# One silu and one product for both token tiles of a feed-forward block, with the roundings, sums and transfers around them reordered

## The reference

```python
def swiglu(u, w_in, w_out):
    gate, up = jnp.split(u @ w_in, 2, axis=-1)
    return (jax.nn.silu(gate) * up) @ w_out
...
    h = h + 0.5 * g1 * swiglu(u, ffn_w_in[l, 0], ffn_w_out[l, 0])
    ...
    h = h + g2 * hybrid_mixer(u, ...)
    ...
    h = h + 0.5 * g3 * swiglu(u, ffn_w_in[l, 1], ffn_w_out[l, 1])
```

## Time and profile before

| what | value |
|---|---|
| median of 3 runs | 1303.82 us |
| profiled execution | 1307.19 us |
| its span | 1305.4 us |
| granted TensorE clock, mean | 0.942 |
| TensorE busy | 1192.3 us, 91% |
| VectorE busy | 869.4 us, 67% |
| ScalarE busy | 467.9 us, 36% |
| transfers | 253.70 MB, 194 GB/s in the mean |

### The profile page before, as it was taken

One profiled execution on the slowest core, in us unless ns is written; L12 is line 12 of the kernel. 1 busy time (PEld: TensorE's weight loads), 2 busy tenths in 40 slices (PEclk: granted clock), 3 DMA queues, 4 the chain that ended last, 5 costly groups with the idle time before them and its releaser, 6 DMA issues.

```text
span 1305.4 us, 13525 instructions
## 1 busy us (share of the span) xinstructions
PE 1192.3 (91%) x5163; PEld 891.6 (68%) x5163; DVE 869.4 (67%) x1579; ACT 467.9 (36%) x833; POOL 25.9 (2%) x30
## 2 busy tenths in 40 slices
PE   3889999589989988999987999995998998999998
PEld 2668888456556566888866888872575655788887
DVE  6877776646676677777467687854476776755553
ACT  2434443101154544444344344411112453634441
POOL 7000000000000000000000000000000000000000
PEclk9989999887969998999998999997977899999999
DMA  9898896155511018877348888833653010576641
GB/s 357 287 332 307 313 335 238 45 171 142 185 35 65 33 51 304 297 281 275 126 165 289 311 321 312 311 129 125 150 177 125 33 33 33 194 237 215 216 155 65
DMA packets 153461, 253.70 MB, mean 194 GB/s; under 512 B 9639, under 2 KB 128053, under 8 KB 145205
## 3 DMA queue, kind: packets, MB, share of 16 engines
q1 hardware_dynamic: 152692, 251.53, 56.1%
q10 hardware_dynamic: 704, 1.30, 0.3%
HBM read 251.76 MB, written 1.05 MB: 194 GB/s over the span
## 4 chain that ended last, share of the span: by engine, by line
PE 79%; DVE 10%; DMA 6%; SPq 2%; issue 1%; ACT 1%; DVEq 0%; ACTq 0%
PE ps L581 10%; PE ps L583 10%; PE ps L582 10%; PE ps L686 10%; PE ps L602 7%; PE ps L604 7%; PE ps L606 7%; DMA tall<-in_ffn_w_out_dram 4%; PE ps L564 4%; PE ps L796 2%; PE ps L731 2%; PE ps L593 2%; PE ps L706 1%; PE ps L705 1%; DVE h L1348 1%
## 5 line engine op out<-in xcount | busy, mean ns | idle before, releaser
L581 PE MATMUL ps<-wh,uh 128*128 128x512 f32 x640 | 252.6, 395 | 0.0
L583 PE MATMUL ps<-wlo,uh 128*128 128x512 f32 x640 | 249.5, 390 | 0.0
L582 PE MATMUL ps<-wh,ul 128*128 128x512 f32 x640 | 249.2, 389 | 0.0
L1325 DVE TENSOR_TENSOR wlo<-wide,wh 128x1024 fp32r<-128x1024 f32 x176 | 204.9, 1220 | 6.7 <-ACT wh L953 6.7
L953 ACT CAST wh<-wide 128x1024 fp32r<-128x1024 f32 x176 | 173.2, 1050 | 23.5 <-DMA wide<-in_ffn_w_in_dram 23.5
L686 PE MATMUL ps<-wide,u 128*128 128x512 f32 (+2 forms) x320 | 130.0, 567 | 28.7 <-issue 28.7
L602 PE MATMUL ps<-th,fh 128*128 128x512 f32 x352 | 144.3, 410 | 5.7 <-DVE fl L1360 5.7
L1354 DVE TENSOR_TENSOR tlo<-tall,th 128x1024 fp32r<-128x1024 f32 x104 | 123.3, 1221 | 27.2 <-ACT th L960 26.5
L604 PE MATMUL ps<-th,fl 128*128 128x512 f32 x352 | 141.3, 401 | 0.0
L606 PE MATMUL ps<-tlo,fh 128*128 128x512 f32 x352 | 141.0, 401 | 0.0
L583 PEld LDWEIGHTS ps<-wlo,uh 128*128 128x128 f32 x640 | 120.1, 188 | 25.6
(11 more groups left out here) (255 smaller groups left out, 1371.0 us busy)
## 6 DMA issues: line engine op xcount, KB each, us to landing
wide<-in_ffn_w_in_dram SPq DMA_DIRECT2D x176, 512.0 KB, 5.1
ada<-in_ada_w_dram SPq DMA_DIRECT2D x60, 1024.0 KB, 7.7
tall<-in_ffn_w_out_dram SPq DMA_DIRECT2D x44, 1024.0 KB, 6.4
wide<-in_w_in_dram SPq DMA_DIRECT2D x14, 1024.0 KB, 7.7
tall<-in_w_out_dram SPq DMA_DIRECT2D x8, 1024.0 KB, 7.3
ada<-in_ada_w_dram SPq DMA_DIRECT2D x16, 512.0 KB, 6.0
wide<-in_c_cmp_w_dram SPq DMA_DIRECT2D x4, 1024.0 KB, 10.4
wide<-in_w_in_dram SPq DMA_DIRECT2D x4, 832.0 KB, 8.0
```

The costliest lines, as they stand in the source:

```text
L581: mm(o, uh[:, k, rows_], wh[:, hsl, :, k, :], start=(k == 0), stop=False, skip_group_check=True)
L582: mm(o, ul[:, k, rows_], wh[:, hsl, :, k, :], start=False, stop=False, skip_group_check=True)
L583: i = mm(o, uh[:, k, rows_], wlo[:, s, :, k, :], start=False, stop=(k == KD - 1), skip_group_check=True)
L1325: tt(wlo[:, n % 2, :, ks, :], raw, wh[:, (n + 1) % 2, :, ks, :].bitcast(F32), ALU.subtract)\
```

## The change

Seven edits, all in the order of work; the arithmetic is the same.
1. ScalarE does one silu over both token tiles (128x512), and VectorE one product. Both semaphores rise by 2 at once.
2. ScalarE rounds only the first two quarters of the next `wide` before the silu; the last two, and both tall copies, come behind it.
3. VectorE: likewise. The product stands behind `rest_f`, two wide remainders and an ada step; two wide remainders and both tall ones come behind it, and behind these the rounds of the sums.
4. VectorE reads round 5 behind `rest_f` of the last block, no longer ahead of it. TensorE waits for that at the mixer's start.
5. Each block of a first feed-forward has two ada pieces; 22 and 23 belong to none.
6. SP issues 22 behind the weights of F_LAT and 23 behind those of F_CMPIN.
7. VectorE uses 20 to 23 in the mixer, before it used 21 to 23.

```diff
@@ -90,7 +90,7 @@
 ADAW = 2 * DM
 ADA_F0, ADA_F1 = 3 * KD, 2 * KD
 ADA_L = ADA_F0 + ADA_F1
-F0_PIECES = [(0, 1), (2, 3), (4, 5), (6, 7), (8, 9), (10, 11), (12, 13), (14, 15, 16), (17, 18), (19, 20), (21, 22, 23)]
+F0_PIECES = [(0, 1), (2, 3), (4, 5), (6, 7), (8, 9), (10, 11), (12, 13), (14, 15), (16, 17), (18, 19), (20, 21)]
 ROUNDS = (6, 6)
 ROUND_AT = {NPAIR - 3: (0, 1), NPAIR - 2: (2, 3), NPAIR - 1: (4, 5)}
 NB = NPAIR
@@ -423,9 +423,6 @@
                             ada_f1(l, b, c)
                     if b + 1 < NB:
                         ffn_tall(l, f, b + 1)
-                    if f == 0:
-                        for n in F0_PIECES[b][2:]:
-                            ada_f0(l, n)
                     if b == 2 and l and f == 0:
                         sp.wait_ge(h_ready, norm_at(l - 1, 2, 3))
                         gate_bias(l, 0, 2 * DM)
@@ -480,9 +477,11 @@
                 n = WIDE_M
                 fill_wide(l, n, [cols(n, 0, 512, 720, 416), cols(n, 208, 720, 928, 416)],
                           (gu_ready, gu_at(l, 0, NB - 2, 1)))
+                ada_f0(l, 3 * KD - 2)
                 n += 1
                 fill_wide(l, n, [cols(n, 0, 1440, 1696, 320), cols(n, 256, 2208, 2272, 320)],
                           (gu_ready, gu_at(l, 0, NB - 1, 1)))
+                ada_f0(l, 3 * KD - 1)
                 n += 1
                 fill_wide(l, n, [cols(n, 256, 256, 512, 512), cols(n, 0, 0, 256, 512)],
                           (proj, projected(l, F_LAT)))
@@ -752,6 +751,7 @@
                          down_done if k % 2 and part == parts - 1 else None, quarters)
 
             def mixer(l):
+                pe.wait_ge(mod_red, rounds_at(l, 0, ROUNDS[0] - 1))
                 for hf in range(2):
                     gate_row(3 * DM + hf * 512, 2 + hf)
                 keep_warm(8)
@@ -976,17 +976,16 @@
                     if b:
                         round_f(l, f, b - 1)
                     if b + 1 < NB:
-                        for c in range(4):
+                        for c in range(2):
                             round_wide(l, f, b + 1, c)
-                    if b:
-                        for a in range(2):
-                            round_tall(l, 2 * f, 2 * b + a)
                     act.wait_ge(gu_ready, gu_at(l, f, b, 1))
-                    for t in range(NT):
-                        A(fs[:, t, :], ps[:, gu_bank(b, t), 0:SEQ], ACT.Silu).then_inc(silu_ready, 1)
-                    if b == 0:
-                        for a in range(2):
-                            round_tall(l, 2 * f, a)
+                    g = gu_bank(b, 0)
+                    A(fs[:, :, :], ps[:, g:g + NT, 0:SEQ], ACT.Silu).then_inc(silu_ready, 2)
+                    if b + 1 < NB:
+                        for c in range(2, 4):
+                            round_wide(l, f, b + 1, c)
+                    for a in range(2):
+                        round_tall(l, 2 * f, 2 * b + a)
                 round_f(l, f, NB - 1)
                 if f == 1 and not last:
                     for c in range(4):
@@ -1409,28 +1408,28 @@
                     if b:
                         rest_f(l, f, b - 1)
                     if b + 1 < NB:
-                        for c in range(4 if b else 2):
+                        for c in range(2):
                             rest_wide(l, f, b + 1, c)
                     if b:
                         for n in pieces[b - 1][1:]:
                             ada_step(l, f, n)
-                        for a in range(2):
-                            rest_tall(l, j, 2 * b + a)
-                    for t in range(NT):
-                        dve.wait_ge(silu_ready, ff_at(l, f, b, t, 2))
-                        tt(fa[:, t, :], fs[:, t, :], ps[:, gu_bank(b, t), SEQ:2 * SEQ], ALU.mult).then_inc(fa_s, 1)
-                    if b == 0:
+                    dve.wait_ge(silu_ready, ff_at(l, f, b, 1, 2))
+                    g = gu_bank(b, 0)
+                    tt(fa[:, :, :], fs[:, :, :], ps[:, g:g + NT, SEQ:2 * SEQ], ALU.mult).then_inc(fa_s, 2)
+                    if b + 1 < NB:
                         for c in range(2, 4):
                             rest_wide(l, f, b + 1, c)
-                        for a in range(2):
-                            rest_tall(l, j, a)
+                    for a in range(2):
+                        rest_tall(l, j, 2 * b + a)
                     for r in ROUND_AT.get(b, ()):
-                        if r < rounds:
+                        if r < min(rounds, 5):
                             mod_round(l, f, r)
                     if b < NB - 1:
                         for n in pieces[b][0:1]:
                             ada_step(l, f, n)
                 rest_f(l, f, NB - 1)
+                if rounds == 6:
+                    mod_round(l, f, 5)
                 if f == 1 and not last:
                     for c in range(2):
                         rest_wide(l + 1, 0, 0, c)
@@ -1462,7 +1461,7 @@
                 for hf in range(2):
                     dve.wait_ge(mod_ps, rounds_at(l, 0, ROUNDS[0] + hf))
                     gate_part(1, hf, 2 + hf).then_inc(mod_red, 1)
-                for n in F0_PIECES[NB - 1]:
+                for n in range(F0_PIECES[NB - 1][0], 3 * KD):
                     ada_step(l, 0, n)
                 dve.wait_ge(s_small, (l + 1) * 160)
```

## The result

The changed kernel takes 1258.82 us (median of three, 1258.26 to 1260.21) for 1303.82 before: 45 us faster by the medians; the ratio of the timed runs is 0.9664, 3.4% faster, 95% interval 0.9626 to 0.9703. The profiled execution took 1260.21 us, its span 1258.4 us for 1305.4: 47.0 less. Behind edit 1 the lines of TensorE and VectorE carry numbers that are 1 to 3 lower.

The account below looks back on a forecast made before the run. TensorE carries 79% of the chain of waits, so its waits were summed: gains 51.6 less 7.0 lost, net 44.6 off the profiled 1307.19 us, 1262.6; less a 3.4 offset, 1259 us, range 1245 to 1279.

Parts of the forecast that it names:

- Joining: One silu and one product over both token tiles of a block, beside TensorE's matmuls: value 0.
- The product ahead of the tall rounding: Block 1 of each of four feed-forwards: shorter TensorE waits for the product, 15.8 us gained, plus 1.6 of clock.
- The rounds: Blocks 8 and 9: the sums are read behind more remainders, so TensorE waits 0.85 or 1.2 us; 7.0 us lost.
- Rival A: The rounds' short waits and one for the second projection each cost the clock: 16 us less gain, 1275; chance 0.16.
- Round 5: Feed-forward ends: `fl` ready earlier, 3.7 us gained at each first one, 0.6 in layer 0's second; sum 8.0.
- The projection weights: Mixers: first projection's weights no longer stand behind late ada pieces; 13.1 us gained per mixer, 26.2 in two.
- B: Mixers: the second projection's weights become the new wait, over 4 us; 1267 us; chance 0.12.
- C: No wait at the second projection or for `lat`, ada pieces earlier in block 1: 1246 us; chance 0.12.
- D: Slower: rounding behind the product delays the next gate-up, in 40 blocks; 1370 us; chance 0.03.
- E: Block 1: the ada piece lands after the old product time, the waits stay; 14 us less, 1273; chance 0.05.

Follow-up runs that it names:

- pieces-alone kernel: The kernel before with only the changes to the ada pieces and SP's queue: 1278.53 us, ratio 0.9808.

## Why the prediction was right

It was right in the time and, place by place, in the mechanism. That 1259 met 1258.82 to 0.2 us is luck: the gain foretold was 2.4 us too small (44.6 for 47.0 of the profiled execution), and the 3.4 us by which I took the median below the profiled execution were 1.4. Inside the 47.0 errors of up to 4.6 us cancel as well. Step by step:

**Joining: 0.** Right, shown from both sides. What the change is named after is not what it gives.

**The product ahead of the tall rounding: 17.4.** It was 21.96: right in the mechanism, too small by 4.6 us. The waits foretold were 1.35, 1.25, 2.9 and 0; they were 2.33, 1.12, 2.99 and 0. In the first feed-forward the ada piece landed at 68.72 (VectorE's step starts there) and not at 67.15, of which 0.7 us is that TensorE too came there later. The term that was mis-sized is the clock. I priced it at some seven matmuls, 1.6 us a wait, and took it back in one stage only; the stages gained 7.1 us beyond their waits (21.96 - 14.86). Two things were wrong. Before, all twelve matmuls of the half down product behind the wait ran at 0.43 us in F1 and F3, and about five in F2 and F4: against the 28.16 us of a stage without a wait, that is 3.1, 1.8, 3.0 and 1.7 us beyond the waits. And a shorter wait need not bring the low clock: the transposes behind the wait of 2.33 us took 0.66 us, where behind 5.85 us they took 1.12, and no matmul behind it or behind the 1.12 us ran at 0.43. Part of this is chance. Blocks 0 to 2 of F1 to F4 sum to 120.0 to 122.8 us in the seven profiles with the new order and the old place of the ada step, and to 142.9 to 144.1 in the four with the old order.

**The rounds: -7.0.** It was -7.25, with waits of 0.6 and 1.0 us in the places named and none in block 10. With the reading moved ahead of the tall remainders all of it went, so these were the cause. My 0.85 us for block 8 was 0.1 more than its own times give (6.85 - 6.1). Rival A, that these waits cost the clock as well, did not come true: the granted clock is 1.00 from 175 to 213 us. Blocks 2 to 9 lose 2.13 us in each of three feed-forwards, where the two waits make up 1.63. The other 0.5 us are not clock. The profile counts a wait from the modelled end of the matmul before it, 0.39 us behind its start, while the next would have started 0.23 us behind it: 0.16 us more a wait. The first matmul behind a wait takes up to 0.1 us longer to the next start (0.53 for 0.43 in block 8, 0.17 for 0.11 in block 9). In block 8 that is 0.61 + 0.16 + 0.10 = 0.87 us, in block 9 1.02 + 0.16 + 0.06 = 1.24.

**Round 5: 8.0.** It was 8.04, and the 0.6 us in F2 had the reason given. But of the 3.7 in F1 and F3 only 2.1 come each time, 31.26 to 29.15. The other 1.6 are low clock behind the 1.89 us wait, and that was chance: the ends of F1 and F3 had it in four of eight cases with the old place of round 5 (twice in this profile of before), and in none of eighteen with the new one. So the edit is worth 2.1 to 3.7 us there. So too the 1.05 us lost in block 0 of F3: TensorE, done earlier, stands 3.64 us for 2.15 ahead of the transposes, and these took 3.68 us for 2.67, but with round 5 alone moved they took 1.97 behind the same wait. I had put this place at nothing.

**The projection weights: 26.2.** It was 25.75. The first projection started with the transposes' end and at full rate (11.34 us for 32 matmuls). The second waited 2.44 and 2.51 us for 1.8 foretold, and low clock behind that wait, which I had only in the bounds, took 1.7 us more. By my working `lat` would be 2.4 us late (276.9 for the end of the transposes at 274.5). It was in time, since TensorE was itself later. The two errors cancelled, which is luck; where the clock stayed up, in the second mixer of the pieces-alone kernel, `lat` was indeed waited for, 1.11 us.

**The other rivals.** B asked for a wait of over 4 us at the second projection, which was not there, though the low clock that it prices was. C asked for no wait there, and there were two. D had nothing: there is no wait ahead of the gate-up matmuls in any block behind 1. E fell with the waits for the product, 21.3 to 6.4 us.

## What to carry to other kernels

Ask of each instruction in an in-order list who waits for it and how soon, and put those that nobody needs for ten microseconds behind those that TensorE needs next; then look at what the moved work now stands ahead of (here a bank's reading, 7 us lost, and all to be had back). A transfer queue is such a list too: a piece that must wait for a compute step blocks all that is behind it, and moving the issue of two pieces gave more here than all reordering of the engines. Look also at what is issued just ahead of a transfer: with 1.3 MB of weights taken out from between two pieces, the second one was used 2.8 us earlier.

## What the runs showed of the hardware

Whether a wait of about 2 us lowers TensorE's clock is not told by its length. In front of the last down product of F1 the kernel before and the pieces-alone kernel do the same and wait the same 1.89 us. Behind it the first ran at the half-rate level, the second did not. Here is TensorE's row of the second, to be held against the last one of the earlier trace rows, and then the window of 231 to 242 us of the kernel before and of the pieces-alone kernel (columns as in the earlier trace rows, the clock third from the end):

```profile
236.29 0.47 PE L601 MATMUL ps<-th,fh 128*128 128x512 f32 x1 [1.89 <-DVE fl L1359]
```
```profile
231.00:242.00 11.00, 9.11 (x38) 7.21 (x37) 4.71 (x12) 1.31 (x3) 0.00 (x0) 0.84 0.00 0
```
```profile
231.00:242.00 11.00, 9.11 (x44) 7.19 (x43) 6.18 (x14) 2.04 (x5) 0.00 (x0) 1.00 0.03 9
```

The end of F1 took 32.87 us in the one and 31.26 in the other: 1.6 us by the clock alone. The same happened inside one execution. In the pieces-alone kernel the second projection waits 2.53 us in one mixer and 2.63 in the other, and takes 10.54 us in the first and 8.85 in the second:

```profile
263.03 10.54 PE L685 MATMUL ps<-wide,u 128*128 128x320 f32 x32 [2.53 <-DMA wide<-in_w_in_dram]
...
888.90 8.85 PE L685 MATMUL ps<-wide,u 128*128 128x320 f32 x32 [2.63 <-DMA wide<-in_w_in_dram]
```

Over all profiles, length tells only the extremes. Ahead of the product's transposes in block 1 there are eleven waits of 0.65 to 1.99 us, and no matmul just behind them ran at the half rate of 0.43 us. Behind two of the three from 2.10 to 2.33 us none did either, behind the third, 2.10 us, eight did. Of the 23 waits from 2.46 to 7.46 us only one, 2.94 us, was followed by none. Of the twelve waits of 1.88 or 1.89 us for `fl` four were followed by seven or eight. The prediction set the 0.61 us of the first matmul behind such a wait against 0.39; the figure to set beside it is the 0.47 us of the pieces-alone kernel, at full clock.

So 1.6 to 1.7 us a wait come and go between executions. In the 30 timed runs of the kernel before that stand beside the experiments, the four with times from 1298.93 to 1300.03 us have a mean granted clock of 0.949, the slowest, 1307.47 us, has 0.942; one run of 1300.68 us with 0.943 does not fit. That the clock is all of the spread was not shown. The two short waits in blocks 8 and 9, 0.6 and 1.0 us, never lowered it: blocks 2 to 9 of F1, F2 and F3 last 122.40 to 122.44 us in all seven profiles that have them.
